# Rates among the first features, a nonlinearity ahead of the gates, and transposes ahead of a mean square, in a state-space stage

## The reference, cut to what matters

```python
def odd_features(h, w_in, conv_w, conv_b, dt_bias):
    z, xbc, dt = _split(h @ w_in, ODD_SIZES)              # 2048, 3072, 64 columns
    xs, bm, cm = _split(jax.nn.silu(dwconv1d(xbc, conv_w, conv_b)), (D_INNER, SSD_BC, SSD_BC))
    dt = jax.nn.softplus(dt + dt_bias)
    ...
def ssd_scan(x, dt, bm, cm, s0, with_out, A):             # one direction, chunks of 128 tokens
        cum = jnp.cumsum(dtc * A, axis=1)
        w_end = jnp.exp(c_end[:, None] - cum) * dtc
        s_new = exp(c_end) * s + einsum('bsgh,bsgn,bsghp->bghpn', w_end, bc, xc)
        cb = jnp.einsum('btgn,bsgn->btsg', cc, bc)
        w = jnp.exp(seg) * cb[..., None] * dtc[:, None]
        y = einsum('btsgh,bsghp->btghp', w, xc) + exp(cum) * einsum('btgn,bghpn->btghp', cc, s)
    ...
def combine(f, y):
        y = y + d_skip * f['x']
        y = y * jax.nn.silu(f['z'])
        y = rmsnorm(y, norm_g)                            # over the 512 features of a group
        return y @ w_out
```

## Time and profile before

| | us |
|---|---|
| median of 3 runs | 3105.27 (3104.22 to 3106.03) |
| the profiled execution | 3109.24 |
| its span in the profile | 3107.4 |
| PE busy | 2791.2 (90%) |
| DVE busy | 1874.8 (60%) |
| ACT busy | 1034.5 (33%) |
| the state-space stage, first item to last mean square | 2418.7 to 2794.8 |

### The profile page before, as it was taken

How to read it: one execution, slowest core, us unless ns; L and a number is a source line. 1 busy time by engine, 2 the same in 40 slices (tenths; PEclk the granted TensorE clock), 3 DMA queues, 4 the chain that set the end, 5 groups by cost and what they waited for, 6 DMA issues and landing times.

```text
span 3107.4 us, 47661 instructions
## 1 busy us (share of the span) xinstructions
PE 2791.2 (90%) x18018; PEld 2348.9 (76%) x18018; DVE 1874.8 (60%) x3213; ACT 1034.5 (33%) x1334; POOL 197.8 (6%) x89
## 2 busy tenths in 40 slices
PE   2999999999999998999799467999999799969998
PEld 2998877999998887899688344587745567648887
DVE  5785254677785844657482675577733576662881
ACT  1432132443542123243433542333301544441211
POOL 0000000000000000000044000144300000000000
PEclk9999999999999998999899579999999999979999
DMA  7786633577673932456151101122252211103441
GB/s 267 269 320 253 231 109 141 203 263 281 222 274 129 342 123 84 175 188 240 66 211 55 63 1 63 67 95 94 83 219 111 82 68 68 55 14 122 150 173 70
DMA packets 109673, 469.59 MB, mean 151 GB/s; under 512 B 7020, under 2 KB 60856, under 8 KB 62136
## 3 DMA queue, kind: packets, MB, share of 16 engines
q1 hardware_dynamic: 109496, 467.19, 41.6%
HBM read 466.10 MB, written 1.06 MB: 150 GB/s over the span
## 4 chain that ended last, share of the span: by engine, by line
issue 52%; PE 30%; DVE 8%; DVEq 6%; ACT 3%; ACTq 1%; POOLq 0%; PEldq 0%; PEld 0%
PE accs L786 9%; DVEq L2570 3%; PE accs L674 3%; DVE arena L2547 2%; PE accs L687 2%; PE accs L689 2%; PE accs L688 2%; PE accs L1134 2%; PE accs L1135 2%; PE accs L1136 2%; DVE normed L86 1%; ACT arena L76 1%; PE mix L1182 1%; DVE arena L86 1%; PE mix L833 1%
## 5 line engine op out<-in xcount | busy, mean ns | idle before, releaser
L687 PE MATMUL accs<-normed_r,arena_r 128*128 128x256 f32 (+2 forms) x1864 | 585.6, 314 | 20.4 <-DVE cond_panel_r L86 6.1
L688 PE MATMUL accs<-arena_r 128*128 128x256 f32 (+1 forms) x2090 | 594.8, 285 | 0.0
L689 PE MATMUL accs<-normed_r,panel_r 128*128 128x256 f32 (+2 forms) x1872 | 585.0, 312 | 0.0
L674 PE MATMUL accs<-normed,panel 128*128 128x256 f32 x2176 | 483.8, 383 | 6.7 <-ACTq L469 3.0
L674 PEld LDWEIGHTS accs<-normed,panel 128*128 128x128 f32 x2176 | 413.9, 192 | 71.3 <-issue 4.6
L86 DVE TENSOR_TENSOR panel_r<-panel,arena_r 128x1024 fp32r<-128x1024 f32 (+1 forms) x240 | 319.7, 1332 | 130.5 <-ACTq L1380 91.2
L688 PEld LDWEIGHTS accs<-arena_r 128*128 128x128 f32 x2090 | 395.5, 189 | 2.2 <-issue 0.2
L687 PEld LDWEIGHTS accs<-normed_r,arena_r 128*128 128x128 f32 (+1 forms) x1864 | 351.2, 188 | 56.4 <-issue 13.0
L1379 ACT ACTIVATE arena_r<-panel 128x1024 fp32r<-128x1024 f32 (+1 forms) x240 | 275.3, 1147 | 303.4 <-PE accs L689 114.6
L689 PEld LDWEIGHTS accs<-normed_r,panel_r 128*128 128x128 f32 (+1 forms) x1872 | 350.8, 187 | 23.9
L2547 DVE SCALAR_TENSOR_TENSOR arena<-accs,vectors,arena 128x189 f32<-128x189 f32 (+2 forms) x704 | 279.3, 428 | 95.2 <-issue 66.0
(11 more groups left out here) (373 smaller groups left out, 4151.8 us busy)
## 6 DMA issues: line engine op xcount, KB each, us to landing
panel<-w SPq DMA_DIRECT2D x250, 1024.0 KB, 4.9
panel<-w SPq DMA_DIRECT2D x48, 1408.0 KB, 7.8
cond_panel<-wc SPq DMA_DIRECT2D x56, 1024.0 KB, 7.0
normed<-wc SPq DMA_DIRECT2D x48, 1024.0 KB, 7.5
arena<-wc SPq DMA_DIRECT2D x16, 1024.0 KB, 5.7
residual<-xs SPq DMA_DIRECT2D x2, 1024.0 KB, 8.3
residual<-crows SPq DMA_DIRECT2D x2, 512.0 KB, 8.8
arena<-cond_row_kept SPq DMA_DIRECT2D x2, 512.0 KB, 6.8
```

What stands on the lines that cost most here:

```text
L674: mm = pe.matmul(acc[b][:, o:o + ntok], w[:, k * PANEL + j * P:k * PANEL + j * P + P], rhs(k), start=(k == 0), stop=(k == KD - 1))
L687: pe.matmul(out, hi[:, k, 0:m], src_hi(k), start=clear and k == 0, stop=False, skip_group_check=True)
L688: pe.matmul(out, hi[:, k, 0:m], src_lo(k), start=False, stop=False, skip_group_check=True)
L689: mm = pe.matmul(out, lo[:, k, 0:m], src_hi(k), start=False, stop=last and k == n - 1, skip_group_check=True)
```

## The change

1. **Rates.** PE runs items 0 to 9 before it transposes the rates, and then items 10 to 15; the `stage_end` is gone on all engines. On DVE the low halves 2 and 3 go in front of most of the rates' chain, and two convolutions with the low halves 4 and 5 in front of its last step. ACT evacuates halves 0 and 1 and copies 4 and 5 before `dt_end`, and halves 2 and 3 with copies 6 and 7 behind it.
2. **First Silu.** ACT applies the first Silu right behind the sixth evacuation, ahead of the gates' evacuations (z) and the next group's four copies. Those four copies now stand behind it.
3. **Between groups.** ACT applies the Silu of B and C ahead of the square, and signals `ssd_conv` there. PE transposes the next x first and does the mean square behind the C.B products, into bank 2 of `mix`. The copy of bank 0 is gone: ACT takes the root from PSUM. On DVE CB now comes ahead of XW, and XW waits for the mean square. PE waits for `ssd_gstd` ahead of the states.
4. **Items in the loop.** Steps 0 to 4 keep two items each; items 13, 14 and 15 stand one each in steps 5, 6 and 7, where before step 5 had two, step 6 one and step 7 none.

The diff, cut to its core:

```diff
@@ PE, ssd_mean_square and ssd_group
-                    mm = pe.matmul(mix[:, 0, 0:T], ones_g[:, :], S_SQ[:, c, :], ...)
+                    mm = pe.matmul(mix[:, 2 if g < 3 else 0, 0:T], ones_g[:, :], S_SQ[:, c, :], ...)
                 if g >= 1:
-                    ssd_mean_square(g - 1)
                     pe.wait_ge(S("ssd_yz"), g)
                 pe.wait_ge(S("ssd_conv"), g + 1)
...
                 mm.then_inc(S("ssd_cb"), 1)
+                if g >= 1:
+                    ssd_mean_square(g - 1)
                 if g < 3:
                     ssd_item(g + 1, 1)
                     ssd_item(g + 1, 2)
                 pe.wait_ge(S("ssd_cb_sb"), g + 1)
                 pe.wait_ge(S("ssd_xw"), g + 1)
+                if g >= 1:
+                    pe.wait_ge(S("ssd_gstd"), g)
...
-                        for item in (2 * m + 3, 2 * m + 4):
-                            if item < 16:
-                                ssd_item(g + 1, item)
+                        for item in (2 * m + 3, 2 * m + 4) if m < 5 else (m + 8,):
+                            ssd_item(g + 1, item)
@@ PE, the stage
-                    for n in range(4):
-                        ssd_item(0, n)
-                    ssd_rates()
-                    for n in range(4, 6):
-                        ssd_item(0, n)
-                    stage_end(pe, count)
-                    for n in range(6, 16):
-                        ssd_item(0, n)
+                    for n in range(16):
+                        ssd_item(0, n)
+                        if n == 9:
+                            ssd_rates()
@@ ACT, ssd_rates
+                for q in range(2):
+                    ssd_features(0, q)
+                    ssd_high(0, q + 4)
                 act.wait_ge(S("dt_end"), 1)
                 act.activation(dwe[0:64, :], dwe[0:64, :], ACT.Exp).then_inc(S("dt_wend"), 1)
-                for i in range(4, 6):
-                    ssd_high(0, i)
+                for q in range(2, 4):
+                    ssd_features(0, q)
+                    ssd_high(0, q + 4)
@@ ACT, ssd_group
-                    act.activation(S_STD, S_STD, ACT.Sqrt, bias=eps_rms).then_inc(S("ssd_gstd"), 1)
+                    act.wait_ge(S("ssd_gms"), g)
+                    act.activation(S_STD, mix[:, 2, 0:T], ACT.Sqrt, bias=eps_rms).then_inc(S("ssd_gstd"), 1)
...
                     act.wait_ge(S("ssd_cv"), g + 2)
-                    act.activation(S_XC[(g + 1) % 2], S_XC[(g + 1) % 2], ACT.Silu)
+                    act.eng.activation(S_XC[(g + 1) % 2], S_XC[(g + 1) % 2], ACT.Silu)
+                    for v in S_BCC[(g + 1) % 2]:
+                        act.eng.activation(v, v, ACT.Silu)
+                    act.drain().then_inc(S("ssd_conv"), 1)
                 act.wait_ge(S("ssd_yz"), g + 1)
                 act.activation(S_SQ[:, :, :], S_Y[:, 4 * g:4 * g + 4, :], ACT.Square).then_inc(S("ssd_gsq"), 1)
-                if g < 3:
-                    for v in S_BCC[(g + 1) % 2]:
-                        act.eng.activation(v, v, ACT.Silu)
-                    act.wait_ge(S("ssd_gms"), g + 1)
-                    act.activation(S_STD, mix[:, 0, 0:T], ACT.Copy).then_inc(S("ssd_conv"), 1)
@@ ACT, the stage
-                    stage_end(act, count)
-                    for q in range(8):
-                        ssd_features(0, q)
...
+                    for q in range(4, 6):
+                        ssd_features(0, q)
+                        ssd_high(0, q + 4)
                     act.wait_ge(S("ssd_cv"), 1)
                     ... Silu of x, B and C, as before ...
+                    for q in range(6, 8):
+                        ssd_features(0, q)
+                        for i in range(2):
+                            ssd_high(1, 2 * (q - 6) + i)
@@ DVE, ssd_rates and ssd_group
                 dve.drain().then_inc(S("dt_onep"), 1)
+                for i in range(2, 4):
+                    ssd_low(0, i)
...
+                for q in range(2):
+                    ssd_conv(0, q)
+                    ssd_low(0, q + 4)
                 dve.wait_ge(S("dt_wend"), 1)
                 dve.tensor_tensor(we, we, d64[:, 0:T], ALU.mult)
                 dve.drain().then_inc(S("dt_rows"), 1)
-                for i in range(2, 6):
-                    ssd_low(0, i)
```

32 lines of the change are left out of this document (13 added, 19 removed).

## The result

| | before | after |
|---|---|---|
| median, runs side by side | 3111.81 us (3104.22 to 3120.31, 7 runs) | 3095.69 us (3087.43 to 3098.78, 7 runs) |
| ratio | | 0.9941, 95% interval 0.9924 to 0.9958 |
| the same pair, measured again | 3114.01 us (11 runs) | 3097.23 us (6 runs), ratio 0.9937 (0.9921 to 0.9954) |
| profiled execution, its span | 3109.24, 3107.4 us | 3098.78, 3096.8 us |
| first item to last mean square (start to start) | 372.31 us | 356.91 us |

The change makes the kernel faster by 0.6%. The predicted ratio was 3089.7 / 3109.24 = 0.9937, inside the interval. The predicted time, 3085.8 us with a range of 3077 to 3093, was too low: the median is 3095.69. 4.0 of the 4.1 lie at the seams between groups.

What follows compares the result with a forecast made beforehand. TensorE's waits at the state-space stage's seams were taken as the bound. Gains of 14.0 + 1.7 + 1.7 + 2.1 = 19.5 us took 3109.24 to 3089.7, or 3085.8 for the median; range 3077 to 3093.

Steps and rivals of the forecast that it cites:

- The sum: Whole stage: 14.0 + 1.7 + 1.7 + 2.1 = 19.5 us gained.
- First seam: Stage start up to group 0: ten items ahead of the rates gain 14.0 us, between 12 and 16.
- Rivals 2 and 5: 2: wait moves, 4 to 10 us lost, chance 0.08; 5: bank or half late, seam stays, about 3103, chance 0.04.
- First seam between groups: Group 0 to 1: transposes earlier, mean square behind C.B products at 1.8 us; 1.7 us gained.
- Second seam: Group 1 to 2: the same gain as at the seam before it, 1.7 us.
- fits in the wait of 4.6: Step 7 between groups: item 15, 2.9 us, is hidden by the wait for the last step's weights.
- step (b): Seams between groups: last three projection halves spread over three steps; all behind DVE's step 6 moves up by 0.7 us.
- Last seam: Group 2 to 3, no items to hide behind: 2.1 us gained; 0.4 with the mean square at half clock.
- Rival 1: Item 8 and seams: the clock holds through the short waits; gains of 22.5 to 29, about 3080; chance 0.18.
- Rival 3: Seams: clock rises late, 1.8 us each at two, 1.7 at the last; gain 12 to 17.5, about 3091; chance 0.19.
- Rival 4: Groups 1 and 2: half clock from the transposes on; all matmuls 66 us, 3152; half of them 3119; chance 0.04.

Runs made afterwards that it cites:

- extra matmuls: The changed kernel plus ten 128x128 matmuls, results never read, behind each group's last products; stage 352.45 us, median 3090.34 us, ratio 0.9928 to the kernel before.
- both: The changed kernel with Silus ahead of evacuation and copies, gate product ahead of last low halves, rates' chain reordered on DVE; 3071.48 us, ratio 0.9874 to before.

## Why the prediction was right or wrong

**The level of the kernel before** was the first error. The sum was carried over to a median of three runs, 3105.27; that kernel's later medians lie between 3109.85 and 3114.01. (The 3111.81 above is a median of seven that takes in those first three; the other four lie between 3111.81 and 3120.31.) What failed is the step that takes 4.0 off the profiled 3109.24 and 3089.7, down to the median, 3085.8. The predicted ratio times 3111.81 is 3092.3 us, 3.4 under what was measured. The range was built from the costs of the edits alone, and left out that 2400 us of untouched code begin the stage anywhere within 12 us. Of the 9.9 us between 3085.8 and 3095.69, 6.5 are this level, and 3.4 are gain that did not come.

**First seam: right.** Predicted 14.0, measured 14.25 to the transposes of B. Step by step: wait at item 8 predicted 3.9, measured 3.72; low clock for items 8 and 9 predicted 1.8 us, measured 1.6 (from item 8 to the rates' transposes 7.17 us, against 5.54; the first seven matmuls are slow); no wait for the rates; Silu ready 4.9 us ahead of PE, predicted 5; transposes warm and the next step 5.2 us behind their start, as predicted (2480.75 - 2475.54 = 5.21). Rivals 2 and 5 fell here. What I had not asked is whether the wait had to be there at all.

**First seam between groups: mechanism right, 0.4 us short.** The transposes came 68.2 us behind the states instead of 73.2: 5.0 earlier, as predicted. From them to the states it took 14.89, not 14.5: the item between them took 3.40 us, not 3.01 as before, as the clock rose only during its first two matmuls (0.78 and 0.53 us, then 0.39).

**Second seam: predicted 1.7, measured -0.2.** The step that failed is that item 15 "fits in the wait of 4.6", "that wait hides it". It was costed at full clock. Here it took 4.62 us instead of the 3.12 of the first seam, at a granted clock of 0.64 behind a wait of 2.00 us, and ACT's evacuation waited 1.19 us for it, so the transposes came 3.9 us earlier instead of 5.0 (without it in step 7, 0.4 us sooner still, step (b)'s 0.7 already lost). The item behind them took 3.78 us and lost 0.8 more. The prediction also took the second seam for a copy of the first ("as much at the second seam"); the profile of before had the two within 0.4 us of each other (84.40 and 84.79), but with the change the waits ahead of the last products differ, and the clock in them.

**Last seam: predicted 2.1, measured 0.4.** The term mis-sized is the mean square at 1.8 us; it took 3.44, at the low clock. The prediction named that value ("with the mean square at half clock 0.4") and chose the other one. The transposes themselves came 5.2 us earlier (predicted 5.4).

**Rivals.** Rival 1 (the clock holds) did not come about. Its prices for single steps bear out: 1.8 for item 8 (1.6 measured), 1.5 for a burst of transposes (1.7 and 1.4 with extra matmuls), 2.8 for the last state products (6.45 before, 3.67 in "both"). Its total, 22.5 to 29, was not reached by this order: with extra matmuls it gave 19.9, since they held the clock at two seams of three and the state products went slow instead. Rival 3 (the clock rises late) is the one whose time, 3091, lay nearest, and the gain of 15.4 us is in its span of 12 to 17.5. Its mechanism holds in part. At the last seam it is what happened. At the first two it is not: the items behind the transposes lost 0.4 and 0.8 us, not 1.8 each. That was the price of a rule in the Trainium skill, TensorE: Matmul & The Clock Gate, Part 4 (PE-mode transpose), that transposes don't count as busy time like matmuls. The trace doesn't agree: a burst that began near half clock (3.65 us) was followed by matmuls at full length from the third one on at the first seam (0.78, 0.53, then 0.39 us), where behind the wait at item 8, with no burst between, seven were slow. Rival 4, half clock throughout groups 1 and 2, did not occur: from 2560 to 2637 us the granted clock was 0.98, from 2645 to 2717 it was 1.00. It did come in the last group, which the rival left out (0.57, and 0.71 before), and there it cost next to nothing.

**My theory after the result** fell in the main. I blamed item 15's place in ACT's queue, and ACT did wait for it (1.19 and 2.08 us at the second and the last seam); but taking it out of step 7 made the stage 2.2 us longer, since step 7's weights then came later. At the two middle seams what also held the Silus, and DVE's gate product beside them, were the copies and low halves written ahead of them, in the kernel before as in the one after.

## What to carry to other kernels

At a seam, list for the engine that releases it everything written ahead of the step that is waited for, and move what the seam doesn't need behind it, on every engine that ends near the same time: here copies and an evacuation on ACT together with low halves on DVE. In "both" the three seams together came out 10.1 us shorter for it, 8.4 of them ahead of the transposes, where moving the waiter's own work had given 1.5. Cost work behind a wait at both clocks, also behind one of 2 us, and let the range hold both. Split a seam at the step that is released: a gain behind it, where nothing was reordered, is the clock's. And take the level, and its spread, from many runs before a median is used as an origin: the parts of a change that lies in one stage are read from the stage, which repeated to 0.33 us in two profiles of one kernel, while its whole times spread over 12.
